# Gated delta rule in one decoder step: state product ahead of the solve, tile 0 in 32x32 blocks, sampled states by one 32-token block per product

## The reference

```
decay = exp(where(causal, gc[:, None] - gc[None, :], -inf))
kb, vb = k * beta, v * beta
m_mat = eye + (kb @ k.T) * decay * strict               # unit lower triangular
sol   = solve(m_mat, [vb, kb * exp(gc)])                # -> u, w
att   = (q @ k.T) * decay
v_new = u - w @ S
o     = (q * exp(gc)) @ S + att @ v_new
S     = S * exp(g_last) + (k * exp(g_last - gc)).T @ v_new
```

## Time and profile before

| | before |
|---|---|
| median of three executions | 1171.08 us (1171.01 to 1173.23) |
| the profiled execution | 1173.02 us |
| its span in the trace | 1171.2 us, 22442 instructions |
| TensorE matmul / weight load busy | 1156.0 us (99%) / 1128.2 us (96%) |
| VectorE / ScalarE / GpSimd busy | 763.9 (65%) / 523.6 (45%) / 63.2 (5%) |
| TensorE's mean granted clock, of full speed | 0.995 |

### The profile page before, as it was taken

The page is one execution under the profiler, slowest core; times in us unless marked ns, Lnnn a source line. Parts: engine busy times, 40 slices in busy tenths (PEclk is TensorE's granted clock), DMA queues, the critical chain, the costliest instruction groups (busy, mean ns, idle before and its releaser), DMA issues.

```text
span 1171.2 us, 22442 instructions
## 1 busy us (share of the span) xinstructions
PE 1156.0 (99%) x9544; PEld 1128.2 (96%) x9544; DVE 763.9 (65%) x1119; ACT 523.6 (45%) x841; POOL 63.2 (5%) x48
## 2 busy tenths in 40 slices
PE   9999999999999999999999999999999999999997
PEld 9999999999999999899999778999999999999997
DVE  6987565767667553476657766455975667675664
ACT  6445334435435443333276555342453434353454
POOL 0000000000000210000013300310000000000003
PEclk9999999999999999999999999999999999999999
DMA  5322312122213332127120012323223122223222
GB/s 196 116 80 99 108 64 100 64 100 90 105 58 109 91 119 76 57 67 74 55 96 2 3 75 95 96 72 91 85 79 108 64 100 91 96 85 109 73 73 81
DMA packets 39219, 99.59 MB, mean 85 GB/s; under 512 B 12112, under 2 KB 15568, under 8 KB 39120
## 3 DMA queue, kind: packets, MB, share of 16 engines
q1 hardware_dynamic: 38064, 95.80, 25.9%
q10 hardware_dynamic: 1056, 2.36, 0.5%
HBM read 92.71 MB, written 5.44 MB: 84 GB/s over the span
## 4 chain that ended last, share of the span: by engine, by line
PE 94%; DVE 2%; ACT 2%; issue 1%; POOLq 0%; DVEq 0%; POOL 0%; DMA 0%; SPq 0%; ACTq 0%
PE ps L894 35%; PE ps L861 22%; PE ps L810 21%; PE ps L1006 9%; PE ps L1427 4%; PE ps L774 1%; PE ps L1441 1%; DVE w_lo L2061 1%; ACT x_hi L1509 1%; DVE h L2123 1%; PE ps L965 0%; PE ps L976 0%; PE ps L1030 0%; PE ps L1119 0%; ACT w_hi L1476 0%
## 5 line engine op out<-in xcount | busy, mean ns | idle before, releaser
L894 PE MATMUL ps<-x_hi,s_hi 128*128 128x296 f32 (+1 forms) x576 | 171.4, 298 | 0.2
L894 PE MATMUL ps<-x_hi,s_lo 128*128 128x296 f32 (+1 forms) x576 | 170.9, 297 | 0.0
L894 PE MATMUL ps<-x_lo,s_hi 128*128 128x296 f32 (+1 forms) x576 | 170.5, 296 | 0.0
L810 PE MATMUL ps<-x_hi,w_hi 128*128 128x296 f32 (+1 forms) x608 | 136.2, 305 | 0.3 <-DVE x_lo L2066 0.3
L810 PE MATMUL ps<-x_lo,w_hi 128*128 128x296 f32 (+1 forms) x608 | 132.5, 299 | 0.0
L810 PE MATMUL ps<-x_hi,w_lo 128*128 128x296 f32 (+1 forms) x608 | 132.2, 299 | 0.0
L894 PE MATMUL ps<-t_hi,s_hi 128*128 128x296 f32 (+1 forms) x432 | 128.4, 297 | 0.0
L894 PE MATMUL ps<-t_hi,s_lo 128*128 128x296 f32 (+1 forms) x432 | 128.2, 297 | 0.0
L894 PE MATMUL ps<-t_lo,s_hi 128*128 128x296 f32 (+1 forms) x432 | 127.9, 296 | 0.0
L2160 DVE TENSOR_TENSOR s_lo<-s_sum,s_hi 128x1024 fp32r<-128x1024 f32 x72 | 88.2, 1225 | 44.5 <-ACT s_hi L1496 41.5
L894 PEld LDWEIGHTS ps<-x_hi,s_hi 128*128 128x128 f32 x576 | 108.4, 188 | 0.6 <-issue 0.6
(11 more groups left out here) (339 smaller groups left out, 2444.2 us busy)
## 6 DMA issues: line engine op xcount, KB each, us to landing
raw<-weights SPq DMA_DIRECT2D x150, 512.0 KB, 3.6
raw<-weights SPq DMA_DIRECT2D x16, 384.0 KB, 3.5
S<-states SPq DMA_DIRECT2D x1, 2048.0 KB, 10.7
new_state<-S ACTq DMA_DIRECT2D x1, 2048.0 KB, 7.4
y_t<-h SPq DMA_DIRECT2D x4, 336.0 KB, 2.3
h<-x_t SPq DMA_DIRECT2D x4, 296.0 KB, 4.2
h<-x_t SPq DMA_DIRECT2D x2, 592.0 KB, 6.8
raw<-weights SPq DMA_DIRECT2D x4, 256.0 KB, 4.5
```

The lines of the kernel that those rows point to most:

```text
L810: last = nc.tensor.matmul(ps[:, slot if out is None else out, half, 0:w_half], w[:, slot, k, :], x[:, k, a:a + w_half], start=(k == 0 and ...
L894: last = nc.tensor.matmul(out, w[:, k, :], x[:, k, :], start=(start and k == 0 and r == 0), stop=(k == KT // 2 - 1 and r == 2), skip_group ...
```

## The change

- **State ahead of the solve.** `end`, `KBG` and `NWT` go. GpSimd makes `EK` = exp(gc)·k for tiles 1 to 4 too, features first. `scan` now is: step 0 EK·S, step 1 VectorE rhs = v - that (beta is in the decay factors), step 2 inverse·rhs and q·S, step 3 ScalarE copies VN, step 4 K·VN and then VN·att, step 5 square, new state, gate, steps 6 to 8 the norm.
- **Tile 0 in blocks of 32, 32 and 16 tokens.** Its levels run like the others' levels 1 to 3, with 12 products of up to 32x32 and VectorE's transposes, one group instead of two. The solve is 12 block products instead of 4.
- **Sampled states.** The sampled states are stored in another sequence (`PLACED`), so that tokens 0 to 31 hold two sequences, 32 to 63 four and 64 to 79 two. GpSimd spreads over 4 copies instead of 8, 80x512. A head's update is three products of 256, 512 and 256 columns, each of one block of tokens.
- **Inverses of tiles 3 and 4** have buffers of their own, whose zero parts are filled again.
- **The order** is another string; the 8 pieces `out_half` are steps of their own (stream o, `half`).

```diff
-FLIPS = [3, 1, 4, 2, 5]
 ORDER = (
-    "ppqpqppppaqqttqapbgggaagzqabagagqaggabaabfazqpzzabpabaapfababaabfaqfbapbabfaqbpfbafbqapbafbaqbqaqz"
-    "afbaztaatfpcababapabspcabppbsabzbzabanpsbpabsabtasbasbababssasbabstbaasbtcbtssbaassasawsshacaassas"
-    "sshshwshswwss"
+    "pzzpqppzppqqzqatqapqqtbpagggbggzfgggaababaabpabapbfbqpapbafqfbpafbqbaapffqbabqfaabqbqzfbacbzaafbas"
+    "cszpabsssbabsabatanstsbbabpabsbspsapbasspspbtpsbababasbtabaasssbastbaabacswsatassaocaswasssaswaohs"
+    "sshsohohssosoowo"
 )
+PLACED = (0, 1, 6, 7, 2, 3, 4, 5)
         def inverse(t):
-            return XY[t % 2][0:TILES[t][1], 1]
+            return XY[t % 2][0:TILES[t][1], 1] if t < 3 else INV[t % 2]
+        def blocks_of(t):
+            return QUARTERS if t else QUARTERS[0:2] + (slice(HALF_P, MAIN),)
 # TensorE, low and up (levels 1 to 4)
-                if t == 0:
-                    for hd in range(2 * q, 2 * q + 2):
-                        last = mm(half_bank(a + q, 0, n)[:, hd - 2 * q, :], AT[p][0:n, hd, 0:n], XY[p][0:n, 0, hd, 0:n])
                 else:
                     for hd in range(H):
-                        for r in QUARTERS:
+                        for r in blocks_of(t):
                             last = mm(block_cols(a)[r, hd, :], AT[p][r, hd, r], x_blocks(t)[r, hd, :])
-            def end(t, i):
-                ...
-                for hd in range(H):
-                    last = mm(heads(a, n)[:, hd, :], KBG[p][0:n, hd, :], inverse(t)[:, hd, 0:n])
-                last.then_inc(s["wt_ps"], 1)
-                for hd in range(H):
-                    last = mm(bank(b)[0:n, hd * P:(hd + 1) * P], inverse(t)[:, hd, 0:n], U_[p][0:n, hd, :])
-                last.then_inc(s["u_ps"], 1)
             def scan(t, i):
                 if i == 0:
-                    pe.wait_ge(s["nwt_ready"], t)
+                    pe.wait_ge(s["ek_ready"], t + 1)
                     ...
                     for hd in range(H):
-                        last = mm(bank(6)[0:n, hd * P:(hd + 1) * P], NWT[p][:, hd, 0:n], S[:, hd, 0, :])
+                        last = mm(bank(6)[0:n, hd * P:(hd + 1) * P], EK[t - 1][:, hd, 0:n], S[:, hd, 0, :])
+                    last.then_inc(s["ks_ps"], 1)
+                if i == 2:
+                    pe.wait_ge(s["rhs_ready"], t + 1)
+                    pe.wait_ge(s["y_ready"][p][0], inverse_done(t))
+                    for hd in range(H):
+                        last = mm(bank(6)[0:n, hd * P:(hd + 1) * P], inverse(t)[:, hd, 0:n], U_[p][0:n, hd, :])
                     last.then_inc(s["vn_ps"], 1)
-                if i == 2:
                     pe.wait_ge(s["qg_ready"], t + 1)
                     for hd in range(H):
-                        mm(heads(7, n)[:, hd, :], S[:, hd, 0, :], EG[:, (t + 1) % 4][:, hd, 0:n], stop=False)
-                        last = mm(heads(7, n)[:, hd, :], VN[0:n, hd, :], ATT[t % 4][0:n, hd, 0:n], start=False)
-                    last.then_inc(s["o_ps"], 1)
+                        mm(heads(7, n)[:, hd, :], S[:, hd, 0, :], EG[:, (t + 1) % 4][:, hd, 0:n], start=hd == 0, stop=False)
+                if i == 4:
+                    pe.wait_ge(s["vn_ready"], t + 1)
+                    pe.wait_ge(s["att_ready"], t + 1)
                     for hd in range(H):
                         last = mm(bank(6)[:, hd * P:(hd + 1) * P], KG[p][0:n, hd, :], VN[0:n, hd, :])
                     last.then_inc(s["s_ps"], 1)
+                    for hd in range(H):
+                        last = mm(heads(7, n)[:, hd, :], VN[0:n, hd, :], ATT[t % 4][0:n, hd, 0:n], start=False)
+                    last.then_inc(s["o_ps"], 1)
 # TensorE, first: solve of tile 0 (i == 3) and state updates (i >= 7)
                     for hd in range(H):
-                        last = mm(bank(7)[0:n, hd * P:(hd + 1) * P], inverse(0)[:, hd, 0:n], u_of(0)[0:n, hd, :])
+                        for r in blocks_of(0):
+                            last = mm(bank(7)[r, hd * P:(hd + 1) * P], y_blocks(0)[r, hd, 0:r.stop - r.start], u_of(0)[r, hd, :])
-                    for half in range(2):
-                        last = mm(bank(6 + half), kg_of(0)[0:n, hd, :], VX[hd % 2][:, 512 * half:512 * (half + 1)])
-                    last.then_inc(s["s4_ps"], 1)
+                    x, (r0, r1, r2) = VX[hd % 2], blocks_of(0)
+                    mm(bank(6)[:, 0:2 * P], kg_of(0)[r0, hd, :], x[r0, 2 * P:4 * P]).then_inc(s["s4_early"], 1)
+                    mm(bank(7), kg_of(0)[r1, hd, :], x[r1, 0:4 * P]).then_inc(s["s4_ps"], 1)
+                    pe.wait_ge(s["s4_early"], hd + 1)
+                    mm(bank(6)[:, 2 * P:4 * P], kg_of(0)[r2, hd, :], x[r2, 0:2 * P]).then_inc(s["s4_ps"], 1)
 # ScalarE: the copies of end go, VN comes
-                nc.scalar.activation(NWT[p][:, :, 0:n], heads(a, n), ACT.Copy, scale=-1.0).then_inc(s["nwt_ready"], 1)
-                nc.scalar.copy(U_[p][0:n], heads(b, P)[0:n]).then_inc(s["u_ready"], 1)
+                    nc.scalar.copy(VN[:], heads(6, P)).then_inc(s["vn_ready"], 1)
 # VectorE: tok, start, scan
-                    V.tensor_tensor(KBG[p][0:n], heads(4, P)[0:n], over_cols(f_cum[0:n, t, :], P), ALU.mult)
-                if t == 1 or t == 2:
+                if t:
                     V.memset(inverse(t)[HALF_P:P, :, 0:HALF_P], 0.0)
                     ...
-                    V.tensor_tensor(VN[:], U_[p][:], heads(6, P), ALU.add).then_inc(s["vn_ready"], 1)
+                    V.tensor_tensor(U_[p][:], U_[p][:], heads(6, P), ALU.subtract).then_inc(s["rhs_ready"], 1)
 # GpSimd: prep 5 and spread
-                    if t == 0:
-                        G.tensor_tensor(EG[:, 1][:, :, 0:n], e[:, :, 0:n], kv[:, 0:H, c0:c0 + n], ALU.mult)...
+                    ek = EK[t - 1] if t else EG[:, 1]
+                    G.tensor_tensor(ek[:, :, 0:n], e[:, :, 0:n], kv[:, 0:H, c0:c0 + n], ALU.mult).then_inc(s["ek_ready"], 1)
-                G.tensor_tensor(VX[hd % 2].rearrange("p (g c) -> p g c", g=NB),
-                                VN[0:n, hd, :].unsqueeze(1).to_broadcast([n, NB, P]),
+                G.tensor_tensor(VX[hd % 2][:, 0:4 * P].rearrange("p (g c) -> p g c", g=4),
+                                VN[0:n, hd, :].unsqueeze(1).to_broadcast([n, 4, P]),
```

More of the change, by code:

```diff
@@ L213, in delta_schedule @@
              + [(part, t, (l, q)) for l in range(1, LEVELS[t]) for part in ("low", "up", "flip")
-                for q in range(1 if t else 2) if part != "flip" or l < LEVELS[t] - 1]
-             + [("end", t, 0)] for t in range(NT)]
+                for q in range(1) if part != "flip" or l < LEVELS[t] - 1]
+             for t in range(NT)]
     streams = {
@@ L229, in delta_schedule @@
         "w": [("weights", j, 0) for j in range(4)],
+        "o": [("half", j, k) for j in range(2) for k in range(4, 8)],
     }
@@ L274, in shape_masks @@
         block = block.T if l else block
-        if l < 4:
-            a = MASK["levels"].start + l * MAIN
-            m[:, a:a + MAIN] = block[:, 0:MAIN]
         a = MASK["levels32"].start + l * BLOCK
@@ L281, in shape_masks @@
     m[:, MASK["ident32"]] = s % BLOCK == c[:, 0:BLOCK]
-    m[:, MASK["group"]] = seq[:, None] == np.arange(NG)[None, :]
+    m[:, MASK["group"]] = seq[:, None] == np.array([0] + [1 + b for b in PLACED])[None, :]
+    m[:, MASK["eights"]] = s % BLOCK // LB == np.arange(4)[None, :]
     return m
@@ L514, in t_blocks @@
             return T1[t % 2][:, :, 0:BLOCK]
-        def first_mask(l):
-            a = MASK["levels"].start + l * MAIN
-            return mask[0:MAIN, a:a + MAIN]
         def block_mask(l):
@@ L1263, in flip @@
                 p, a, b, base = chain_at(t)
-                if t and l < 5:
+                if l < 5:
                     return
@@ L1396, in first @@
                         pe.wait_ge(s["s4_ready"], hd)
-                    for half in range(2):
-                        last = mm(bank(6 + half), kg_of(0)[0:n, hd, :], VX[hd % 2][:, 512 * half:512 * (half + 1)])
-                    last.then_inc(s["s4_ps"], 1)
+                    x, (r0, r1, r2) = VX[hd % 2], blocks_of(0)
[3 more added lines that the diff above has]
+                    mm(bank(6)[:, 2 * P:4 * P], kg_of(0)[r2, hd, :], x[r2, 0:2 * P]).then_inc(s["s4_ps"], 1)
             def nothing(t, i):
                 pass
-            steps = {"prep": prep, "tok": tok, "start": start, "low": low, "up": up, "flip": flip, "end": end, "scan": scan, "first": first, "states": state_heads,
+            steps = {"prep": prep, "tok": tok, "start": start, "low": low, "up": up, "flip": flip, "scan": scan, "first": first, "states": state_heads, "half": out_half,
                      "silu": nothing, "cast": nothing, "heads": nothing, "weights": nothing, "store": nothing}
@@ L2006, in nothing @@
                 pass
-            steps = {"prep": prep, "tok": tok, "start": start, "low": low, "up": up, "flip": flip, "end": end, "scan": scan, "first": first, "states": nothing,
```

(12 more changed lines are left out.)

225 lines of the change are left out of this document (83 added, 142 removed).

## The result

The change made the kernel slower: 1177.15 us (median of 11 runs, 1172.74 to 1179.12) against 1171.18 us (11 runs, 1170.51 to 1175.11) of the kernel before on the same chip, ratio 1.0042 [1.0032, 1.0052]. The forecast was 1162.1 us.

What follows compares the result with a forecast made beforehand. TensorE was taken to bound the kernel, busy 99% of the span. Its work terms summed to -9.1 us with gaps about unchanged, the walk gave 9.5; a gain of 9.0 took the median from 1171.08 to 1162.1 us, range 1158.0 to 1167.5.

Steps and rivals of the forecast that it cites:

- W products: K·beta·decay through the inverse, in step `end` of tiles 1 to 4: four removed from TensorE, 3.8 us.
- A round of tile 0: TensorE, tile 0's inverse: 24 records take 0.3 us a round, 1.8 in all, so 3.4 us removed.
- Solve of tile 0: TensorE: 12 products of 32x128 instead of 0.94 us for 4 heads, taken as 1.4 us, +0.4.
- A head: Sampled states on TensorE: three block products take 1.2 us instead of 1.92, 0.7 us saved per head.
- -9.1: Sum of TensorE work in the stage, in us: -3.8 - 3.4 + 0.4 - 2.8 + 0.5.
- A: Rival: row blocks do not overlap in the sampled states and tile 0's solve; gain 3.9, 1167.2 us; chance 0.10.
- GpSimd gets 4 more products ... so hidden: EK products of 1.293 us each, +5.2 us on GpSimd, needed only when that tile's scan begins, so hidden.
- part 3's -2.8: Sampled states: 0.7 us a head saved on TensorE by three block products, 2.8 us in all.
- D: Rival: TensorE's gaps lower its clock, 2.9 us an episode, the fourth making it slower: 1173.7 us; chance 0.05.
- B: Rival: latency replaces work, more waits of the two inverse chains come out; gain 5, 1166 us; chance 0.17.
- C: Rival: the gap episode at 684.6 (2.9 us) goes and other gaps are 0.6 lower; 1158.6 us; chance 0.13.
- the forecast's own walk through the waits: Three engines followed through the new order: gaps about 4 us before the first scan, 3 to 4 after; gain 9.5.

Runs made afterwards that it cites:

- e14: The kernel of e5 run once more, on another chip: 1165.78 us, ratio 0.9954 against the kernel before.
- e5: e1 with the sampled states' block products undone (two 512-column products over 80 rows per head, GpSimd spread 80x1024): 1165.48 us, 0.9946 of before.
- e1: The changed kernel, with GpSimd's products of tiles 2 and 4 waiting until VectorE is through its mask operations: 1167.71 us, 0.9966 of before.
- e7: The kernel before with only the sampled-state change (other sequence, 80x512 spreads, three block products per head): 1178.40 us, ratio 1.0053.
- e13: The kernel before, its sampled-state products over the first 32 of 80 rows only, same columns and count: 1179.43 us, ratio 1.0059.
- e2: The changed kernel, with GpSimd's products waiting for VectorE's mask operations at tile 2 alone: 1169.17 us, 0.9986 of before.
- e4: e1 with nine VectorE memsets of 0.3 us into an unused buffer ahead of tile 2's mask operations: 1174.68 us, 1.0036 of before.
- e8: e5 with GpSimd's first two spreads ahead of its products of tile 2: 1170.30 us (1165.44 to 1180.57), 1.0006 of before.
- e9: e8 with the product of EK and the state issued twice in each scan: 1172.39 us (1168.47 to 1181.82), 1.0015 of before.
- e10: e7 with one more product of 384 columns per head over all 80 rows, its result overwritten: 1184.93 us, 1.0106 of before.
- e6: The kernel before with one more 128x512 GpSimd product in tiles 1 to 4, into an unread buffer: 1174.01 us, ratio 1.0022.

## Why the prediction was wrong

**The work was nearly right.** W products gone, as foretold. A round of tile 0: 0.37 against 0.3. Solve of tile 0: 0.99 against 1.4, hardly more than before. A head: 1.37 against 1.2, 0.55 saved instead of 0.7, four times. Four table loads instead of six, as foretold. Together -8.6 us by span times clock (1166.5 to 1157.9), which reads low at after's clock, or -7.3 to -7.8 by e14, e5 and the rows of a head, against -9.1. The factor of up to four that the Trainium skill gives (TensorEngine Tiling (Array Packing), section Theoretical Speedup), which I didn't take, would have given 0.96 a head; the 1.37 us of e1 are not that. A is refuted: the blocks overlap.

**The step that failed first: "GpSimd gets 4 more products ... so hidden".** I priced the cover by who reads the result, and asked neither what the products run beside nor what they hold up. Tiles 2 and 4's products fell on VectorE's mask operations and stretched them from 1.17 to 4.51 and 3.01 us; that, through TensorE's gaps and its clock, is 8.9 us (e1 against after). Two rows of before could have warned, one of VectorE's timeline and one of GpSimd's: an operation that takes 0.29 us elsewhere took 1.37, and ended (644.96) just behind the spread (644.82).

```profile
643.59 1.37 DVE L2595 TENSOR_TENSOR d_inv<-mask,d_t 128x128 f32<-128x128 f32 x1
```
```profile
642.92 1.90 POOL L2836 TENSOR_TENSOR work<-d_v_new,mask 80x1024 f32<-80x1024 f32 x1 [1.84 <-ACT d_v_new L1951]
```

**The step that failed second: part 3's -2.8.** Its work is 2.2 us less by the rows of a head, its time 1.4 to 2.3 us (in the new order) to 7.3 us (in the old) more, since 32-row products lower the clock with no long gap ahead (e7, e13). The prediction put the clock down to gaps alone, and never asked about it in a stretch where almost every product is small.

The two account for the miss: 8.9 + 2.3 + the 2.8 not gained = 14.0 us, against 4.9 + 9.0 = 13.9 from forecast to result, all by ratios (0.0042 x 1171 = 4.9; by the medians, 1177.15 - 1171.18 + 9.0, it is 15.0). Without both, the forecast's own terms give 9.0 - 2.8 = 6.2 us gained; e5 and e14 gained 5.6 and 6.1 by their medians (6.3 and 5.4 by the ratios).

**D came true, half by its own mechanism.** It had gaps of TensorE lowering the clock, decided from the fourth on, at 2.9 us each, and gave 1173.7 us. There were two long gaps, 2.4 and 2.1 us. The price of one was wrong: the slow stretch of before lasted 3.5 us, those behind the gaps of after 10.5 and 11. And part 3 alone loses 10 us at half clock with no gap over 0.5 us ahead (e7). Among forecast, B and C, e5 and e14 speak for the forecast's own walk through the waits: their 1165.5 and 1165.8 us lie within 1 us of 1162.1 + 2.8 = 1164.9.

**What stays open.** When a gap lowers the clock and when not (2.12 us did in after and didn't in e2), what makes the short stretches at half with no long gap ahead (633.5 in e4, 633.0 in e8, 644.5 in e13; the 32x32 products of tile 0's rounds stand ahead of the first two), what lets VectorE in between two GpSimd instructions (e8 and e9), and e10's filler. That 32 rows lower the clock is shown by the effect; how is not.

## What to carry to other kernels

Before an operation is put on an idle GpSimd, look at what VectorE does in those microseconds: operations with two operands in SBUF each waited out a GpSimd instruction here, and back-to-back GpSimd instructions can hold one for several. Cutting products to few rows saves TensorE's time and can cost its clock, so take the granted clock of the stretch into the sum, and judge a change by span and clock apart, comparing the product of the two only at like clocks.

## What the runs showed of the hardware that I had not expected

- A VectorE operation with two SBUF operands took 1.1 us instead of 0.29 beside GpSimd instructions of 1.1 to 1.3 us, 2.60 us instead of 0.29 (e6), and 4.35 us across three GpSimd instructions without a pause (e8), but 0.72 in the same place of e9. Memsets beside them did not stretch.
- The same products, columns and count over 32 rows instead of 80 run at the same speed (1.88 and 1.92 us) until the granted clock falls to half for 17.5 us (0.59 and 0.56 over 650 to 660 and 660 to 670), with TensorE busy 98% and more.
- Three products of 256, 512 and 256 columns on three sets of 32 rows that share all output columns take 1.37 us, 0.71 of the same columns over 80 rows.
- One kernel can give 1165 and 1180 us in turn by the clock alone (e8: 0.997 and 0.984), with span times clock within 0.12% of itself. That steadiness isn't general: the runs of before spread by 0.3% in it.
